# Norm weights stored as 128 equal rows, and the first token tile turned behind one weight unit instead of two

## The reference

```python
def rms_norm(x, w):
    xf = x.astype(F32)
    y = xf * lax.rsqrt(jnp.mean(xf * xf, axis=-1, keepdims=True) + EPS)
    return (y * w.astype(F32)).astype(x.dtype)
...
for layer in range(DEPTH):
    y = rms_norm(h, nw[0])
    y = even_mixer(y, ...)        # layer 0: proj = y @ w_in, attention and a recurrent part, @ w_out
    h = h + rms_norm(y, nw[1])
    y = conv_ffn(rms_norm(h, nw[2]), ...)
    h = h + rms_norm(y, nw[3])
```

## Time and profile before

| | us |
|---|---|
| median of 3 runs | 1133.23 |
| fastest and slowest of them | 1131.72, 1135.26 |
| the profiled execution | 1134.19 |
| its span, first to last instruction | 1132.4 |

### The profile page before, as it was taken

One profiled execution on the slowest core, in us unless ns is written; L12 is line 12 of the kernel. 1 busy time (PEld: TensorE's weight loads), 2 busy tenths in 40 slices (PEclk: granted clock), 3 DMA queues, 4 the chain that ended last, 5 costly groups with the idle time before them and its releaser, 6 DMA issues.

```text
span 1132.4 us, 18318 instructions
## 1 busy us (share of the span) xinstructions
PE 1100.3 (97%) x7632; PEld 1011.0 (89%) x7632; DVE 714.7 (63%) x1101; ACT 563.6 (50%) x934; POOL 71.1 (6%) x80
## 2 busy tenths in 40 slices
PE   5999999999999999999999999999999999999998
PEld 4988879999988889889999887889999989999986
DVE  5766575877755556767667555955555795555651
ACT  5744455655644444546556444437433835444540
POOL 3220001000001000010000001221000000000000
PEclk9998999999999999999999999999999999999999
DMA  7842345655555544256555556663333446555550
GB/s 290 296 152 75 112 146 207 209 184 180 187 191 179 224 156 141 96 194 222 186 185 184 189 169 210 197 225 130 113 113 111 138 143 217 174 186 186 184 188 37
DMA packets 56530, 195.53 MB, mean 173 GB/s; under 512 B 6656, under 2 KB 9600, under 8 KB 56448
## 3 DMA queue, kind: packets, MB, share of 16 engines
q1 hardware_dynamic: 56448, 194.37, 51.3%
HBM read 193.29 MB, written 1.05 MB: 172 GB/s over the span
## 4 chain that ended last, share of the span: by engine, by line
PE 88%; DVE 4%; ACT 4%; POOL 2%; issue 1%; DMA 1%; SPq 0%; ACTq 0%; DVEq 0%
PE ps L927 42%; PE ps L863 27%; PE ps L1172 3%; PE ps L1057 3%; PE ps L1011 3%; PE ps L988 2%; DVE lo L1363 2%; PE ps L1000 1%; ACT pr L566 1%; PE ps L938 1%; POOL ms L499 1%; PE ps L1090 1%; PE ps L1233 1%; DMA raw<-in_weights 1%; PE ps L957 1%
## 5 line engine op out<-in xcount | busy, mean ns | idle before, releaser
L1363 DVE TENSOR_TENSOR lo<-raw,hi 128x1024 fp32r<-128x1024 f32 (+2 forms) x346 | 412.6, 1218 | 100.3 <-ACT hi L553 99.3
L927 PE MATMUL ps<-y_hi,hi 128*128 128x256 f32 x1360 | 387.3, 285 | 0.0
L553 ACT ACTIVATE hi<-raw 128x1024 fp32r<-128x1024 f32 (+2 forms) x346 | 347.1, 1035 | 80.4 <-DMA raw<-in_weights 80.3
L927 PE MATMUL ps<-y_hi,lo 128*128 128x256 f32 x1360 | 384.8, 283 | 0.0
L927 PE MATMUL ps<-y_lo,hi 128*128 128x256 f32 x1360 | 384.7, 283 | 0.0
L927 PEld LDWEIGHTS ps<-y_hi,hi 128*128 128x128 f32 x1360 | 260.9, 192 | 1.0 <-issue 0.7
L927 PEld LDWEIGHTS ps<-y_lo,hi 128*128 128x128 f32 x1360 | 260.9, 192 | 0.0
L927 PEld LDWEIGHTS ps<-y_hi,lo 128*128 128x128 f32 x1360 | 260.8, 192 | 0.0
L863 PE MATMUL ps<-hi,h_hi 128*128 128x512 f32 x296 | 91.8, 391 | 0.6 <-DVE h_lo L1775 0.6
L863 PE MATMUL ps<-hi,h_lo 128*128 128x512 f32 x296 | 92.2, 393 | 0.0
L863 PE MATMUL ps<-lo,h_hi 128*128 128x512 f32 x296 | 91.8, 391 | 0.0
(11 more groups left out here) (274 smaller groups left out, 1438.5 us busy)
## 6 DMA issues: line engine op xcount, KB each, us to landing
raw<-in_weights SPq DMA_DIRECT2D x346, 512.0 KB, 4.1
gain<-in_gains SPq DMA_DIRECT2D x11, 512.0 KB, 6.9
bias<-in_rel SPq DMA_DIRECT2D x16, 128.0 KB, 2.1
h<-in_x SPq DMA_DIRECT2D x2, 512.0 KB, 6.5
mem_x<-in_mem SPq DMA_DIRECT2D x2, 512.0 KB, 14.7
out<-h SPq DMA_DIRECT2D x2, 512.0 KB, 2.6
pick<-in_c_pick SPq DMA_DIRECT2D x1, 512.0 KB, 8.4
hw<-in_hgrn_w SPq DMA_DIRECT2D x1, 256.0 KB, 5.8
```

Of the source, the lines that this page charges most:

```text
L553: act.activation(hi[:, s, :w], raw[:, s, :w], ACT.Copy).then_inc(hi_done, 1)
L927: mm = pe.matmul(dst, w[:, s, at], x(k), start=first and k == 0, stop=final and k == nk - 1)
L1363: dve.tensor_tensor(lo[:, s, :w], raw[:, s, :w], hi[:, s, :w].bitcast(F32), ALU.subtract).then_inc(lo_done, 1)
```

## The change

The gains are repeated 128 times on the host, so that the tensor in HBM is 11 x 128 x 1024, and each load reads 128 rows in a row instead of one row 128 times. The bytes written to SBUF and the number of rows per transfer (128 of 4 KB) are the same. At the start, ACT and DVE no longer make the parts of unit 0 and 1 and then those of tile 0, but unit 0, tile 0, unit 1. For tile 1 the DVE loop's text changes too, but `units(4)` has nothing left to do there and its order stays. PE, POOL and SP run the same instructions in the same order.

```diff
     return {
-        "weights": weights, "gains": gains, "conv": conv, ...
+        "weights": weights, "gains": np.repeat(gains[:, None, :], P, 1), "conv": conv, ...
...
-                sp.dma_start(gain[:, g % 2, :], dram["gains"][g:g + 1, :].partition_broadcast(P)).then_inc(gain_in[g % 2], 16)
+                sp.dma_start(gain[:, g % 2, :], dram["gains"][g]).then_inc(gain_in[g % 2], 16)
...
             square_tokens(0, 0, h, (x_in[0], 16), (x_in[0], 16))
+            units(1)
+            turned_hi(0, 0, y_hi, (0,))
             units(2)
-            turned_hi(0, 0, y_hi, (0,))
             square_tokens(0, 1, h, (x_in[1], 16), (x_in[1], 16))
...
                 norm(0, 0, t, h)
+                units(3 * t + 1)
+                turned_lo(0, 0, y_lo, y_hi, (t,))
                 units(2 * t + 2)
-                turned_lo(0, 0, y_lo, y_hi, (t,))
```

More of the change, by code:

```diff
@@ L194, in lay_out @@
     return {
-        "weights": weights, "gains": gains, "conv": conv, "head_gains": head_gains, "rows_in": rows_in,
+        "weights": weights, "gains": np.repeat(gains[:, None, :], P, 1), "conv": conv, "head_gains": head_gains, "rows_in": rows_in,
         "lb": lb, "hgrn_w": a["hgrn_norm_w"], "rel": table, "x": a["x"][0], "mem": a["mem_2"][0],
```

## The result

The changed kernel takes 1138.29 us (median of 9 runs, 1134.88 to 1144.16) against 1133.23 (9 runs, 1130.51 to 1135.59): a ratio of 1.0046, 95% interval 1.0027 to 1.0066. It is slower, by 5.1 us, where I had forecast 2.2 less. Its runs also lie further apart, over 9.3 us and not 5.1.

What follows compares the result with a forecast made beforehand. The prediction took TensorE to bound the kernel, with its restart near the start set by gain 0's landing and the chain behind it. Restart 2.2 us earlier, other terms nothing: 1133.23 - 2.2 = 1131.0 us, range 1128.8 to 1134.2.

Steps and rivals of the forecast that it cites:

- What bounds the kernel: Whole span: chain 88% TensorE, 1% DMA; only an earlier TensorE restart after the start counts, later gain loads nothing.
- Plain rows, L = 5.75: Start: L, gain 0's landing and DVE's first gain multiplication, comes at 5.75 us instead of 8.63, at a unit's pace.
- middle bound of 7.29: Gain 0's landing if only the bytes lost in the slow DMA stretch come back: 552 KB, 1.34 us earlier.
- L + 8.2 for the scaling: Start, new order: DVE scales tile 1 8.2 us after gain 0 lands, at 13.95 instead of 16.13.
- L + 10.9 for the restart: Start: TensorE restarts after the scaling and unit 2's `lo`, at 16.6 us instead of 18.84.
- The moved parts: New order at the start: gives nothing at the restart, which the old order would make about 1 us earlier still.
- The pause of 2.7: TensorE's wait for unit 2 after its first 12 matmuls: 2.7 us instead of 1.46.
- rival A: TensorE restarts at the lower clock after the longer pause, losing 1.6 or 3.2 us: 1132.6 or 1134.2; chance 0.22.
- B: Plain rows at the start land no sooner; the order alone makes the restart 0.7 us later: 1133.9; chance 0.10.
- C: Half the effect at the start: gain 0 lands near 7.3, restart 0.6 us earlier: 1132.6; chance 0.10.
- D: The half-clock stretch at 88 us is shortened or missed, 3.4 us less beside the 2.2: 1127.6; chance 0.08.
- No change within 0.3%: Whole kernel: the result counts as no change, since measurement tells about 0.3%, 3.4 us; chance 0.85.

Runs made afterwards that it cites:

- e2: The kernel before with only the new order of parts at the start, gain loads unchanged: median 1140.9 us, ratio 1.0057.
- e1: The kernel before with only the gains stored as 128 plain rows, old order of parts: median 1133.4 us, ratio 0.9998.
- e3: The changed kernel with 6 useless matmuls in TensorE's first pause, between unit 1 and unit 2: median 1133.2 us, ratio 0.9987.
- e6: The changed kernel with TensorE's first product held back until the parts of unit 1 are there, no work added: median 1133.6 us, ratio 1.0006.
- e12: The kernel before with plain-row gains, old order, and unit 0's load issued ahead of gain 0: 1133.2 us, one run.
- e10: The changed kernel with 12 useless fp32 matmuls at the start of TensorE's queue as a warm-up: 1135.2 us, ratio 1.0013.
- e9: The kernel before, gain 0 still one row, with unit 0's load issued ahead of gain 0: 1137.0 us, one run.

## Why the prediction was wrong, point by point

- *What bounds the kernel.* Right: the nine later gain loads changed nothing that shows, and the span follows the restart, but only with the second number beside it, the time at the lower clock.
- *Plain rows, L = 5.75.* The step that failed first. I took the nearest rows for gain 0's pace. It measured 7.88, and 6.55 to 8.21 in eight more profiles, around the middle bound of 7.29 that I had worked out from the lost bytes and did not take. The GB/s rows were the better witness: they said how much there was to win in all. This step was off by 2.1 us and took away the forecast gain; it does not explain the loss.
- *L + 8.2 for the scaling, L + 10.9 for the restart.* Right: 8.10 and 10.80, within 0.02 of that in the other profiles of the new order without a warm-up. `ms` ended with DVE's multiplication, as assumed.
- *The moved parts.* Right in sign, too large in size: they cost 0.6 us at the restart and not 1.
- *The pause of 2.7.* It was 2.26, longer than before, as said; 2.7 was a slip, too, since 9.9 + 3.76 is 13.7 and leaves 2.9. The first twelve matmuls took 4.21 us (12.21 to 16.42) and not 3.76, as the full clock did not come until 24.1. Here is the main failure: I priced the longer pause at nothing in the forecast, on one row (full pace behind the 2.73 us pause at 69 us), and gave rival A 0.22. The runs showed in its place that the new order puts them at a lower mean granted clock, 5.8 us more lost in e2 than in the kernel before. In the changed kernel the place at 69 us went the other way: behind a pause of 2.96 TensorE ran at half pace, and so it did in five more profiles (e1, e2, e3, e6, e12), where the pause was 2.95 or 2.96, and in e10 behind 2.31; in e9, with 2.82, it did not. One row of one execution was no evidence that pauses are harmless, and no length of the pause parts the two cases.
- *Rival A.* The right mechanism, the lower clock, but its place and price only in part: I priced 1.6 or 3.2 us at the restart. In the changed kernel's profile it cost 2.7 there, and 1.7 more at 72 us, where I did not look for it; e1's restart was slow behind a short pause and e2's was not behind a long one. The Trainium skill's rule on idle gaps (TensorE: Matmul & The Clock Gate, "Why this matters for your kernels") warns of long ones. These runs agree with it in direction, since with the pauses filled the median is 1131.8 and not 1138.3; they do not show that the length decides.
- *Rivals B, C, D.* B's price for the order alone, 0.7, is near what the chain shows (0.6: restart 19.76 against 18.84 with L later by 0.32), and not what the time shows. C was right on L. D did not come: the stretch at 88 us is as long as before, 6.8 us, at 92.4.
- *No change within 0.3%.* Wrong, since I took the clock's states as noise that both kernels share. The change shifted how often they come: a mean granted clock of 0.998 or more in 66 of 104 runs before, and in none of 9 after.

What is shown: the order of parts makes the loss (e2 against e1), the loss is time at the lower clock, and work in TensorE's first pause removes it (e3); a later start of its products points the same way (e6). What stays open: why an execution of one and the same kernel falls to the lower clock at 69 or between 88 and 116 us and another does not, how a pause at 17 us makes that more frequent, and where in the program the runs without a trace lose.

## What to carry to other kernels

Starting TensorE sooner without bringing the next operands sooner only stretched its wait here, and the runs then spent some microseconds more at half clock, part of it much later in the program. Where a reordering lengthens such a wait, try it with a few useless matmuls in the wait before judging the order itself. Judge the edit by many runs, with their spread and their mean granted clocks, as a profile shows only one of the cases. Before pricing a transfer by its neighbour's pace, take the bytes lost in the slow stretch as the bound.

## What the runs showed of the hardware

- One row of 4 KB read for all 128 partitions landed 2.2 us behind the transfer ahead (e9), 128 equal rows 1.3 us (e12), one run each.
- The first large transfer behind `h` and `ident` needed 1.8 to 3.6 us instead of 1.3, with plain rows of the gains or of the weights tensor (eleven profiles).
- Transposes are paced by the clock like matmuls: 8 of them took 1.94 us at the lower level and 1.06 at the higher (e10), and with them the restart came 1.07 nearer to L.
- Half of the time at the lower clock was lost by the span, to within 0.7 us in twelve profiles, whatever TensorE was doing in it.
- The length of a pause alone does not tell the clock behind it. After the same twelve matmuls at half pace TensorE restarted at the lower clock behind 1.01 us (e1) and 2.26 us (changed), at the full one behind 2.27 us (e2).
